# Half-row transposes with one copy per unit, GpSimd's weight split cut by stage, a reversed second branch, and one operation moved from VectorE to ScalarE, in a two-block transformer kernel

## The chip, the cores and the metric

The kernel is one program on one core of a Trainium2 chip. A core has TensorE (PE in the profile; PEld is its weight load), VectorE (DVE), ScalarE (ACT), GpSimd (POOL) and SyncE (SP), which runs the queue of the weight DMAs. The metric is the device time of one execution in microseconds (us). What a measurement of this kernel can tell from no change is about 0.2%, some 4 us.

## The reference

The input is one sequence of 512 tokens with 1024 channels, in float32. Two layers of a first block are followed by one layer of a second.

```python
for l in range(2):                                   # first block
    h = rmsnorm(x, attn_norm[l])
    q, kc, vc, ksl, vsl, kwn, vwn, gts, gq, gk, gv, ga, gr, uv = split(h @ w_in[l])
    o_nsa = gates-weighted sum of three attentions   # compressed, selected, window
    o_gla = gated linear attention(gq, gk, gv, ga, gr)
    o_sg = spatial gating(uv)
    x = x + concat([o_nsa, o_gla, o_sg]) @ w_out[l]
    h = rmsnorm(x, ffn_norm[l])
    x = x + (silu(h @ w_gate[l]) * (h @ w_up[l])) @ w_down[l]
x = rmsnorm(x, final_norm)
h = rms_norm(x, g_pre) * (1 + scl) + shift           # second block
xa, za, q, k, v, zb, ga, gb = split(h @ w_in_2)
y_a = (recurrence(xa) + reversed recurrence(xa)) * silu(za) @ w_pa
y_b = neighbourhood attention(q, k, v) * silu(zb) @ w_pb
x = x + gate * ((sigmoid(ga) * y_a + sigmoid(gb) * y_b) @ w_o)
return rms_norm(x, g_final)
```

With 8 selection blocks and a top-k of at least 8, the selected attention of the first block is a full causal attention, and so is the window attention (the window is 512). Each has 8 heads of 64 channels, and the softmax of each is multiplied by a gate for its row.

## The kernel before

**Weights.** All large products run over a stream of 278 slots of 128x1024 weights (`stream_plan`), in a ring of four (`RING`). SyncE loads a slot into `raw`, GpSimd splits it in two parts that TensorE can multiply in its fast float32 form: `w_hi` is the rounded weight (line 2079, a product with ones), and `w_lo` is what rounding lost (line 2083). The activations are split likewise (`a_hi` by ScalarE, `a_lo` by VectorE at line 1410). A product of a 128x128 weight tile is then three matmuls (lines 402, 405 and 406), and a slot of eight tiles is 24. The first matmul of a slot raises `slot_used`, which frees the slot before it, so GpSimd starts on slot n+4 when TensorE starts on slot n+1. `pieces_of` decides for each turn of the ring: where a slot stands beside much VectorE work, four pieces of 256 columns each for `w_hi` and then for `w_lo`, and else one piece of 1024 columns each. GpSimd's program is written with hardware loops over turns.

**The order of the work.** Nothing is scheduled by a tool. `ORDER`, `BEFORE` and `BESIDE` name, step by step, which projection runs beside which part of the linear attention and of the softmax attention, and each engine runs its program in that order. PSUM has eight banks. `claim` and `room` hand a bank out and make TensorE wait until its last reader has raised `free`. In the projections `aux_bank` takes the banks in turn, first of 4, from "Nh" on of 7 (`pool_of`). The first projection, `gate`, is always in bank 0, and every eviction waits for `rstd`, the factor of the norm, which is ready only when TensorE is through with the first projection and the sum of squares (line 427).

**The first block's attention** runs over 32 units u in each layer: head pair j = u // 8, row block i = u // 2 % 4, and branch u % 2 (selected or window). A unit has w = 128 * (i + 1) keys. For each unit and each of two heads TensorE makes scores (line 641), VectorE the maximum (1620), ScalarE the exponentials (1125), VectorE the scaling by 1/sum and the gate (1669), TensorE a transpose of each 128x128 block (653) in bank 4 (head 0) or 5 (head 1), ScalarE a copy to SBUF (1146), and TensorE the product with v (691), which adds into bank 6 over all eight units of a head pair. TensorE is two units ahead with the scores and one behind with the values. After the last unit of a pair, ScalarE copies bank 6 out (1177), and the next pair's first product (685) waits for that. ScalarE's further work in this loop, the exponentials of the compressed branch (1133) and the activations of other mixers (1170), stands between.

**The gates.** `gN` holds the gates with a row of tokens on each partition. ScalarE writes it (1005), and VectorE then multiplies eight columns by `rowok` (1472), since the first rows have no compressed key.

**The second block** makes its transposes of softmax rows (835) already on halves of 64 rows, the upper into bank 4 and the lower into bank 5.

## Time and profile before

| | |
|---|---|
| median of 3 runs | 2053.39 us (2050.51 to 2055.06) |
| the profiled execution | 2054.61 us, its span 2052.6 us |
| granted clock of TensorE, mean | 0.969 of full speed |
| busy: PE, POOL, DVE, ACT | 94%, 69%, 57%, 30% of the span |
| layer 1 of the first block, from the first evictions to the attention's end | about 729 to 1010 us |

Start and duration in the timeline are in us; "[5.06 <-DVE proj L1504]" says that the engine had stood idle for 5.06 us and what ended that. A row with x8 is eight instructions in one go, and its duration reaches from the first start to the modelled end of the last, so the pace of matmuls is read from one start to the next start. Line numbers are those of the kernel before.

### The profile page before, as it was taken

How to read it: one execution, taken by the hardware profiler on the slowest of the kernel's cores; microseconds unless marked ns; L12 is line 12 of the kernel's file. 1: busy time of each engine (PE TensorE's matmuls, PEld its weight loads, DVE VectorE, ACT ScalarE, POOL GpSimd, SP SyncE). 2: the span in 40 equal slices, each digit the busy share in tenths (PEclk: the TensorE clock that was granted, in tenths of full speed). 3: DMA queues.
4: the chain of work that ended last, by engine and by line, in shares of the span. 5: the costliest groups of instructions: out<-in, count | busy, mean ns of one | idle time of the engine just before them, and what ended most of it. 6: DMA issues, size and time to landing. Idle time of an engine off the chain costs nothing.

```text
span 2052.6 us, 28491 instructions
## 1 busy us (share of the span) xinstructions
PE 1924.2 (94%) x10022; PEld 1489.2 (73%) x10022; DVE 1160.2 (57%) x1670; ACT 615.6 (30%) x1116; POOL 1419.6 (69%) x1208
## 2 busy tenths in 40 slices
PE   7898889999999999988899999997999999989997
PEld 5676557888888877755588888885777777768775
DVE  5765774466257347478556704654937666650353
ACT  4124662210011131266531100113036566540111
POOL 8554117988789985511298978886897878757772
PEclk9999989999999999999999999998999999999998
DMA  5132002343334222300124433542132233222221
GB/s 204 53 96 80 22 11 83 122 143 108 97 121 136 92 72 81 116 21 22 32 93 123 133 100 96 148 124 67 51 108 84 79 94 87 76 72 93 84 91 41
DMA packets 68680, 182.44 MB, mean 89 GB/s; under 512 B 23888, under 2 KB 24144, under 8 KB 68432
## 3 DMA queue, kind: packets, MB, share of 16 engines
q1 hardware_dynamic: 60480, 154.48, 24.8%
q10 hardware_dynamic: 8080, 26.32, 4.1%
q8 instruction: 80, 1.31, 0.3%
q14 instruction: 40, 0.33, 0.1%
HBM read 178.67 MB, written 2.10 MB: 88 GB/s over the span
## 4 chain that ended last, share of the span: by engine, by line
PE 70%; DVE 13%; ACT 7%; issue 6%; POOL 2%; DMA 1%; ACTq 0%; DVEq 0%; POOLq 0%
PE PS L402 21%; PE PS L406 20%; PE PS L405 20%; POOL w_lo L2083 2%; PE PS L691 1%; PE PS L653 1%; PE PS L641 1%; PE PS L441 1%; ACT P L1251 1%; ACT rg L1322 1%; DVE gN L1472 1%; DVE P L1946 1%; PE PS L538 1%; POOL w_hi L2079 1%; DVE PS L1620 1%
## 5 line engine op out<-in xcount | busy, mean ns | idle before, releaser
L2079 POOL TENSOR_TENSOR w_hi<-raw,const 128x256 fp32r<-128x256 f32 (+1 forms) x602 | 641.9, 1088 | 586.1 <-PE PS L402 578.2
L2083 POOL TENSOR_TENSOR w_lo<-raw,w_hi 128x256 fp32r<-128x256 f32 (+1 forms) x602 | 783.9, 1324 | 13.4
L402 PE MATMUL PS<-a_hi,w_hi 128*128 128x512 f32 x1616 | 651.7, 403 | 42.3 <-POOL w_lo L2083 14.1
L405 PE MATMUL PS<-a_lo,w_hi 128*128 128x512 f32 x1616 | 635.8, 393 | 0.0
L406 PE MATMUL PS<-a_hi,w_lo 128*128 128x512 f32 x1616 | 635.3, 393 | 0.0
L402 PEld LDWEIGHTS PS<-a_hi,w_hi 128*128 128x128 f32 x1616 | 307.1, 190 | 128.6 <-issue 46.0
L406 PEld LDWEIGHTS PS<-a_hi,w_lo 128*128 128x128 f32 x1616 | 307.2, 190 | 65.9
L405 PEld LDWEIGHTS PS<-a_lo,w_hi 128*128 128x128 f32 x1616 | 307.6, 190 | 64.8 <-issue 3.4
L1793 DVE TENSOR_TENSOR work<-PS,rstd 128x512 f32<-128x512 f32 x88 | 60.8, 691 | 147.6 <-PE PS L406 140.9
L402 PE MATMUL PS<-f_hi,w_hi 128*128 128x512 f32 x352 | 138.7, 394 | 0.0
L406 PE MATMUL PS<-f_hi,w_lo 128*128 128x512 f32 x352 | 138.0, 392 | 0.0
L405 PE MATMUL PS<-f_lo,w_hi 128*128 128x512 f32 x352 | 136.6, 388 | 0.0
L1216 ACT ACTIVATE work<-work 128x512 f32<-128x512 f32 x44 | 27.8, 633 | 314.4 <-DVE small L1797 314.3
L1849 DVE TENSOR_TENSOR x<-PS,x 128x512 f32<-128x512 f32 x32 | 22.1, 691 | 158.4 <-PE PS L406 158.3
L1804 DVE TENSOR_TENSOR f_lo<-work,f_hi 128x512 fp32r<-128x512 f32 x44 | 85.5, 1944 | 36.9 <-ACT f_hi L1219 36.9
L1219 ACT ACTIVATE f_hi<-work 128x512 fp32r<-128x512 f32 x44 | 27.9, 634 | 205.1 <-DVE work L1800 205.1
L1800 DVE TENSOR_TENSOR work<-work 128x512 f32<-128x512 f32 x44 | 83.5, 1898 | 2.8 <-ACT work L1216 1.4
L653 PEld LDWEIGHTS PS<-const,work 128*128 128x128 f32 x320 | 37.7, 152 | 63.7 <-DVE work L1669 43.3
L653 PE MATMUL PS<-const,work 128*128 128x128 f32 x320 | 58.2, 310 | 24.8 <-DVE work L1669 21.7
L406 PEld LDWEIGHTS PS<-f_hi,w_lo 128*128 128x128 f32 x352 | 66.1, 188 | 15.5
L405 PEld LDWEIGHTS PS<-f_lo,w_hi 128*128 128x128 f32 x352 | 66.1, 188 | 14.8
L1620 DVE CUSTOM_DVE_ANT_0 PS<-PS,before_diag 128x128 f32<-128x128 f32 (+3 forms) x128 | 63.9, 499 | 21.3 <-PE PS L641 17.4
(290 smaller groups left out, 2494.1 us busy)
## 6 DMA issues: line engine op xcount, KB each, us to landing
raw<-weights SPq DMA_DIRECT2D x278, 512.0 KB, 3.5
work<-mod_w ACTq DMA_DIRECT2D x24, 512.0 KB, 3.6
work<-cmp_w ACTq DMA_DIRECT2D x8, 1024.0 KB, 5.6
bias<-rpb SPq DMA_DIRECT2D x256, 12.0 KB
rgw<-rgw ACTq DMA_DIRECT2D x8, 256.0 KB, 2.6
out<-xc SPq DMA_DIRECT2D x8, 256.0 KB, 2.0
const<-const SPq DMA_DIRECT2D x1, 1436.5 KB, 15.3
x<-x_t SPq DMA_DIRECT2D x4, 256.0 KB, 6.8
```

Source lines behind the costliest of these rows:

```text
L402: ins = nc.tensor.matmul(out, wh, hi, start=start, stop=False)
L405: nc.tensor.matmul(out, wh, lo, start=False, stop=False)
L406: return nc.tensor.matmul(out, wl, hi, start=False, stop=stop)
L653: ins = nc.tensor.transpose(PS[:, 4 + hh, n * P:(n + 1) * P], work[:, 2 * br + hh, n * P:(n + 1) * P], ident)
L1216: A(work[:, f % 2, :], work[:, f % 2, :], ACT.Silu).then_inc(to_dve.sem, 1)
L1219: A(f_hi[:, f, :], work[:, 4 + f % 2, :], ACT.Copy).then_inc(h_hi.sem, 1)
L1620: V.tensor_tensor_reduce(s2[:, hh, 0:w], s2[:, hh, 0:w], mask, -1.0, -2 * NEG_MASK, ALU.add, ALU.min, nmax[:, br, hh:hh + 1]).then_inc(max ...
L1793: TT(work[:, w0 + f % 2, :], PS[:, b0 + f % 2, :], rstd[:, :], ALU.mult)\
L1800: TT(work[:, 4 + f % 2, :], work[:, f % 2, :], work[:, 2 + f % 2, :], ALU.mult)\
L1804: TT(f_lo[:, f, :], work[:, 4 + f % 2, :], f_hi[:, f, :].bitcast(F32), ALU.subtract)\
L2079: G.tensor_tensor(w_hi[:, r, k, :], raw[:, r, k, :], ones[:, k, :], ALU.mult).then_inc(pool_chain, 1)
L2083: ins = G.tensor_tensor(w_lo[:, r, k, :], raw[:, r, k, :], w_hi[:, r, k, :].bitcast(F32), ALU.subtract)
```

## The change

- `row_block`: in the window branch (odd u) the row blocks come in reverse. The widths of the units were 1, 1, 2, 2, 3, 3, 4, 4 times 128 and are 1, 4, 2, 3, 3, 2, 4, 1.
- `turn`: each 128x128 transpose is two of 64 rows, the upper into bank 4 and the lower into bank 5. Both heads lie in both banks, one semaphore counts them, and ScalarE copies both banks with one instruction.
- `pool_of["next"] = 0` at the start of each layer.
- The copy of bank 6 stands ahead of the compressed exponentials and the activations in ScalarE's loop.
- The multiplication of `gN` by `rowok` is ScalarE's (a copy with a scale for each partition).
- GpSimd has no loops. `parts_of` gives each slot its pieces, and every piece waits until the one before it is complete: (2, 4), two of `w_hi` with a tensor_scalar and four of `w_lo`; (2, 2), two of each in turn; (1, 1), as before. By the plan 85 slots are (2, 4), 49 are (2, 2) and 144 are (1, 1), where before 108 had four and four and 170 one and one.

```diff
+def row_block(u):
+    i = u // 2 % NT
+    return i if u % 2 == 0 else NT - 1 - i
...
-                pool_of["banks"] = 4
+                pool_of["banks"], pool_of["next"] = 4, 0
...
                     j, i, br = unit(u)
+                    key = (l, "PT", u)
+                    if claim(key, 4):
+                        pe.wait_ge(*room(key))
+                    if u == 0:
+                        pe.wait_ge(free[5], fills[5])
                     for hh in range(2):
                         pe.wait_ge(scaled.sem, scaled.seen_by("pe"))
-                        key = (l, "PT", hh, u)
-                        if claim(key, 4 + hh):
-                            pe.wait_ge(*room(key))
                         for n in range(i + 1):
-                            ins = nc.tensor.transpose(PS[:, 4 + hh, n * P:(n + 1) * P],
-                                                      work[:, 2 * br + hh, n * P:(n + 1) * P], ident)
-                        ins.then_inc(filling(key)[0], 1)
+                            for r in range(2):
+                                q = slice(HD * r, HD * r + HD)
+                                ins = nc.tensor.transpose(PS[:, 4 + r, (2 * n + hh) * HD:(2 * n + hh + 1) * HD],
+                                                          work[q, 2 * br + hh, n * P:(n + 1) * P], ident[q, q])
+                    ins.then_inc(filling(key)[0], 1)
...
-                                                   work[:, 4 + 2 * br + hh, n * P:(n + 1) * P],
+                                                   turned[:, :, (2 * n + hh) * HD:(2 * n + hh + 1) * HD],
...
                         A(gN[:, :, :], PS[:, uses[(l, name, "T")][0], 0:NT * 24].rearrange("p (n c) -> p n c", c=24), ACT.Sigmoid)\
+                            .then_inc(act_chain.sem, 1)
+                        act.wait_ge(act_chain.sem, act_chain.raised())
+                        if l == 0:
+                            act.wait_ge(const_in, 16)
+                        A(gN[:, 0, 2:24:3], gN[:, 0, 2:24:3], ACT.Copy, scale=c_("rowok"))\
                             .then_inc(emptied((l, name, "T")), 1)
...
-                        g = gN[:, 0, 2:24:3]
-                        TS(g, g, c_("rowok"), None, ALU.mult).then_inc(dve_chain.sem, 1)
-                        dve.wait_ge(dve_chain.sem, dve_chain.raised())
...
-                    for hh in range(2):
-                        act.wait_ge(*filling((l, "PT", hh, u)))
-                        A(work[:, 4 + 2 * par + hh, 0:w], PS[:, 4 + hh, 0:w], ACT.Copy)\
-                            .then_inc(emptied((l, "PT", hh, u)), 1)
-                        act.wait_ge(*emptying((l, "PT", hh, u)))
+                    act.wait_ge(*filling((l, "PT", u)))
+                    A(work[:, 4 + 2 * par:6 + 2 * par, 0:w], PS[:, 4:6, 0:w], ACT.Copy)\
+                        .then_inc(emptied((l, "PT", u)), 1)
+                    act.wait_ge(*emptying((l, "PT", u)))
...
+            def split(n, hi_parts, lo_parts):
+                r = n % RING
+                pool.wait_ge(raw_in[r], 16 * (n // RING + 1))
+                if n >= RING:
+                    pool.wait_ge(slot_used, n - RING + 1)
+                each, per = 8 // hi_parts, lo_parts // hi_parts
+                for h in range(hi_parts):
+                    k = slice(h * each, (h + 1) * each)
+                    if hi_parts == lo_parts:
+                        G.tensor_tensor(w_hi[:, r, k, :], raw[:, r, k, :], ones[:, k, :], ALU.mult).then_inc(pool_chain, 1)
+                    else:
+                        G.tensor_scalar(w_hi[:, r, k, :], raw[:, r, k, :], 1.0, None, ALU.mult).then_inc(pool_chain, 1)
+                    pool.wait_ge(pool_chain, counted())
+                    for q in range(h * per, (h + 1) * per):
+                        k = slice(q * 8 // lo_parts, (q + 1) * 8 // lo_parts)
+                        ins = G.tensor_tensor(w_lo[:, r, k, :], raw[:, r, k, :], w_hi[:, r, k, :].bitcast(F32), ALU.subtract)
+                        if q < lo_parts - 1:
+                            ins.then_inc(pool_chain, 1)
+                            pool.wait_ge(pool_chain, counted())
                 ins.then_inc(split_done, 1)
...
+            def parts_of(n):
+                kind, m = PLAN[n][0], PLAN[n][-1]
+                if n == 0 or kind in ("pa", "pb", "wo") or kind == "in2" and not KT <= m < 6 * KT:
+                    return 2, 2
+                if kind in ("in", "in2") or kind == "out" and m < 2:
+                    return 2, 4
+                return 1, 1
```

In the rows of the programs below, a name ahead of the arrow is what is written, and the shape is that of the output. First ScalarE in layer 0, from the copy of unit 16's transposes to that of unit 17's (line 1177, after it 1159, is the copy of bank 6; 1170 and 1180 are the activations). Before:

```order
L1146 ACTIVATE work<-PS 128x128 x2
L1125 ACTIVATE work,sums<-PS,nmax 128x256 x2
L1133 ACTIVATE Pc<-Pc 128x8x31
L1170 ACT_TABLE_LOAD
L1170 ACTIVATE proj<-proj 128x512 x2
L1177 ACTIVATE proj<-PS 128x512
L1146 ACTIVATE work<-PS 128x128 x2
```

After:

```order
L1150 ACTIVATE work<-PS 128x2x128
L1130 ACTIVATE work,sums<-PS,nmax 128x256 x2
L1159 ACTIVATE proj<-PS 128x512
L1138 ACTIVATE Pc<-Pc 128x8x31
L1180 ACT_TABLE_LOAD
L1180 ACTIVATE proj<-proj 128x512 x2
L1150 ACTIVATE work<-PS 128x1024
```

The copy of bank 6 moved ahead of three other operations, two copies became one, and unit 17 is four blocks wide where it was one.

Then TensorE in layer 0, from unit 14's transposes to unit 16's (653 transposes, 691 values, 641 and then 637 scores). Before:

```order
L653 MATMUL PS<-const,work 128x128 x8
L691 MATMUL PS<-work,proj 64x128 x6
L641 MATMUL PS<-keys,proj 128x128 x2
L653 MATMUL PS<-const,work 128x128 x8
L691 MATMUL PS<-work,proj 64x128 x8
L641 MATMUL PS<-keys,proj 128x256 x2
L653 MATMUL PS<-const,work 128x128 x2
```

After:

```order
L653 MATMUL PS<-const,work 128x64 x16
L691 MATMUL PS<-work,proj 64x128 x4
L637 MATMUL PS<-keys,proj 128x512 x2
L653 MATMUL PS<-const,work 128x64 x4
L691 MATMUL PS<-work,proj 64x128 x8
L637 MATMUL PS<-keys,proj 128x256 x2
L653 MATMUL PS<-const,work 128x64 x4
```

Each transpose became two with half the output columns, and the width changes from unit to unit in place of every second one.

Last GpSimd at layer 0's output projection, the slots "out" 6, "out" 7 and the first of the feed-forward part. Before:

```order
L2079 TENSOR_TENSOR w_hi<-raw,const 128x1024 [waits slot_used,raw_in3]
L2083 TENSOR_TENSOR w_lo<-raw,w_hi 128x1024 [waits pool_chain]
L2079 TENSOR_TENSOR w_hi<-raw,const 128x256 [waits slot_used,raw_in0]
L2079 TENSOR_TENSOR w_hi<-raw,const 128x256 x3
L2083 TENSOR_TENSOR w_lo<-raw,w_hi 128x256 [waits pool_chain] x4
L2079 TENSOR_TENSOR w_hi<-raw,const 128x256 [waits slot_used,raw_in1]
```

After:

```order
L2086 TENSOR_TENSOR w_hi<-raw,const 128x1024 [waits slot_used,raw_in3]
L2092 TENSOR_TENSOR w_lo<-raw,w_hi 128x1024 [waits pool_chain]
L2086 TENSOR_TENSOR w_hi<-raw,const 128x1024 [waits slot_used,raw_in0]
L2092 TENSOR_TENSOR w_lo<-raw,w_hi 128x1024 [waits pool_chain]
L2086 TENSOR_TENSOR w_hi<-raw,const 128x1024 [waits slot_used,raw_in1]
```

Four slots of eight pieces each (two are shown in part) are slots of two pieces after the change. The same holds in layer 1.

## Rows read from the trace of the kernel before

**Rows 1.** The page, section 1: busy us, share of the span, instructions.

```profile
PE 1924.2 (94%) x10022; PEld 1489.2 (73%) x10022; DVE 1160.2 (57%) x1670; ACT 615.6 (30%) x1116; POOL 1419.6 (69%) x1208
```

**Rows 2.** Windows: stretch, length, busy of each engine, PEclk, DMA, GB/s.

```profile
26.20:85.26 59.06, 50.27 (x289) 39.06 (x288) 37.46 (x32) 17.90 (x25) 43.63 (x67) 0.89 0.24 72
730.30:778.31 48.01, 47.97 (x287) 37.79 (x288) 24.62 (x31) 13.60 (x19) 39.62 (x56) 0.94 0.23 68
195.00:305.00 110.00, 92.20 (x632) 59.09 (x630) 81.65 (x231) 76.46 (x186) 15.78 (x24) 0.91 0.05 15
1500.00:1835.00 335.00, 323.15 (x1869) 243.90 (x1868) 212.45 (x320) 195.80 (x327) 262.26 (x323) 0.99 0.30 85
```

**Rows 3.** Timeline at layer 1's start, VectorE and TensorE: start, duration, instruction.

```profile
729.39 0.69 DVE L1504 TENSOR_TENSOR proj<-PS,rstd 128x512 f32<-128x512 f32 x1 [5.38 <-ACT rstd L987]
...
730.34 0.76 PE L402 MATMUL PS<-a_hi,w_hi 128*128 128x512 f32 x1 [5.06 <-DVE proj L1504]
...
735.60 0.43 PE L402 MATMUL PS<-a_hi,w_hi 128*128 128x512 f32 x1
...
737.02 0.40 PE L402 MATMUL PS<-a_hi,w_hi 128*128 128x512 f32 x1
```

**Rows 4.** Timeline, the `rowok` operation and what follows, layers 0 and 1.

```profile
41.95 16.55 DVE L1472 TENSOR_SCALAR gN<-gN,const 128x8 f32<-128x8 f32 x1 [0.93 <-ACT gN L1005]
...
55.65 2.82 POOL L2083 TENSOR_TENSOR w_lo<-raw,w_hi 128x256 fp32r<-128x256 f32 x4
...
67.47 1.99 PE L538 MATMUL PS<-work 32*128 32x64 f32 x32 [7.54 <-DVE work L1524]
...
746.86 0.48 DVE L1472 TENSOR_SCALAR gN<-gN,const 128x8 f32<-128x8 f32 x1 [0.95 <-ACT gN L1005]
```

**Rows 5.** Timeline of TensorE: transposes of the first and second block.

```profile
212.74 1.09 PE L653 MATMUL PS<-const,work 128*128 128x128 f32 x8
213.76 1.09 PE L691 MATMUL PS<-work,proj 128*64 128x128 f32 x16
...
1618.50 0.71 PE L835 MATMUL PS<-const,P 64*128 64x64 f32 x16
1619.14 0.50 PE L402 MATMUL PS<-a_hi,w_hi 128*128 128x512 f32 x1
```

**Rows 6.** Waits of TensorE over the span: us in total, times, longest.

```profile
PE PS L685 <- ACT proj L1177: 11.8, 4, 4.3
...
PE PS L402 <- DVE y_lo L2038: 2.9, 2, 1.8
```

**Rows 7.** Timeline of layer 0's unit 16, ScalarE and TensorE.

```profile
254.36 0.60 ACT L1177 ACTIVATE proj<-PS 128x512 f32<-128x512 f32 x1
...
255.01 2.07 PE L685 MATMUL PS<-PTc,vblk 64*128 64x512 f32 x2 [4.29 <-ACT proj L1177]
```

**Rows 8.** GpSimd's groups by shape: busy us, mean ns, idle before.

```profile
L2083 POOL TENSOR_TENSOR w_lo<-raw,w_hi 128x1024 fp32r<-128x1024 f32 x170 | 428.8, 2522 | 13.4
L2083 POOL TENSOR_TENSOR w_lo<-raw,w_hi 128x256 fp32r<-128x256 f32 x432 | 355.1, 853 | 0.0
L2079 POOL TENSOR_TENSOR w_hi<-raw,const 128x1024 fp32r<-128x1024 f32 x170 | 347.4, 2044 | 320.5 <-PE PS L402 318.4
L2079 POOL TENSOR_TENSOR w_hi<-raw,const 128x256 fp32r<-128x256 f32 x432 | 294.4, 712 | 265.6 <-PE PS L402 259.8 <-DMA const<-const 5.8
```

**Rows 9.** Timeline, a VectorE operation beside a piece of 1024 columns.

```profile
1379.18 2.74 POOL L2083 TENSOR_TENSOR w_lo<-raw,w_hi 128x1024 fp32r<-128x1024 f32 x1
...
1379.69 2.79 DVE L1397 TENSOR_TENSOR work<-work 128x512 f32<-128x512 f32 x1
```

**Rows 10.** Timeline at the feed-forward part's start in layer 0.

```profile
357.76 0.69 DVE L1778 TENSOR_TENSOR x<-PS,x 128x512 f32<-128x512 f32 x1 [2.53 <-PE PS L406]
...
361.71 1.11 DVE L1383 TENSOR_TENSOR tmp<-tmp,sq 128x512 f32<-128x512 f32 x1
...
362.97 1.10 PE L427 MATMUL PS<-tmp,const 128*128 128x512 f32 x2
```

More of the change, by code:

```diff
@@ L102 @@
              + [(m, k) for m in range(OUT_EARLY, KT) for k in range(KT)])
-PIECES = 4
-def beside_vector(item):
-    if item[0] == "in2":
-        return item[1] < 6 * KT
-    return item[0] == "in" or item[0] == "gate" and item[2] < 2
+def row_block(u):
+    i = u // 2 % NT
+    return i if u % 2 == 0 else NT - 1 - i
 def stream_plan():
@@ L1172, in _ @@
                             act.wait_ge(to_dve.sem, to_dve.raised())
-                    if u % 8 == 0 and u:
-                        t = u // 8 - 1
-                        act.wait_ge(*filling((l, "O", t)))
-                        A(proj[:, t, :], PS[:, 6, :], ACT.Copy).then_inc(emptied((l, "O", t)), 1)
-                        act.wait_ge(*emptying((l, "O", t)))
                     if CONVERT_FROM <= u < U - 1:
@@ L2067, in _ @@
             G = nc.gpsimd
+            spent = [0]
             ones = c_("ones")[:, 0:1].unsqueeze(2).to_broadcast([P, 8, P])
-            def split(r, arrival, used, chain, pieces):
-                pool.wait_ge(raw_in[r], arrival)
-                if used is not None:
-                    pool.wait_ge(slot_used, used)
-                each = 8 // pieces
-                for n in range(pieces):
-                    k = slice(n * each, (n + 1) * each)
-                    G.tensor_tensor(w_hi[:, r, k, :], raw[:, r, k, :], ones[:, k, :], ALU.mult).then_inc(pool_chain, 1)
-                for n in range(pieces):
-                    k = slice(n * each, (n + 1) * each)
-                    pool.wait_ge(pool_chain, chain + n + 1)
-                    ins = G.tensor_tensor(w_lo[:, r, k, :], raw[:, r, k, :], w_hi[:, r, k, :].bitcast(F32), ALU.subtract)
-                ins.then_inc(split_done, 1)
@@ L2086, in pieces_of, with counted @@
[L2086 to L2109 removed]
+            def counted():
+                spent[0] += 1
+                return spent[0]
@@ L2112, in _ @@
+            def parts_of(n):
[5 more added lines that the diff above has]
+                return 1, 1
+            pool.wait_ge(head_in, 16)
+            for n in range(SLOTS):
+                split(n, *parts_of(n))
         @block.sync
```

46 lines of the change are left out of this document (14 added, 32 removed).

## The prediction

> **What bounds the kernel now.** I read the page first. TensorE is busy for 94% of the span [rows 1], so the time is TensorE's work, its gaps, and the slower pace behind gaps. Then I read windows by stage. The feed-forward parts are full of TensorE's work, and nothing shorter on another engine helps there. In the second block's main stage TensorE is busy for 323 of 335 us, and GpSimd for 262. In the first block's attention TensorE has 92 of 110 us, VectorE 82 and ScalarE 76 [rows 2]: three engines that hand each unit on to one another, none of them full. Last I followed each gap of TensorE over 2 us to what ended it. Two lie at the starts of the layers and one at each fourth or so of the attention; the rest belongs to serial norms that the change doesn't touch.
>
> A gap costs twice. At layer 1's start TensorE stood for 5.06 us, and the 12 matmuls behind the gap took from 730.34 to 735.60 us, 0.44 us each (the level of 1.2 GHz), while the next six took 1.42 us, 0.24 each (2.4 GHz) [rows 3]. So the gap cost another 12 x 0.20 = 2.4 us.
>
> **Step A, banks reset at layer 1.** The 42 bank picks of a layer leave `next` at 3, so layer 1's second projection gets bank 0, in which the first one still waits for `rstd`. The row shows it: TensorE started right after the eviction of 729.39 [rows 3]. With `next` at 0 it gets bank 1 and needn't wait, as in layer 0. Gain 5.1 + 2.4 = 7.5 us. What is late next is the norm factor itself, which is there 5 us before TensorE is through with the second projection.
>
> **Step B, `rowok` on ScalarE.** In layer 0 this operation on eight columns took 16.55 us, from 41.95 until 58.50, and GpSimd's row of pieces without a gap ended at 58.47; in layer 1 the same operation took 0.48 us [rows 4]. While it stood, evictions and the linear attention's first level stood behind it, and TensorE waited 7.54 us for the latter, at a low clock behind that [rows 4]. To price it I compare the same stretch of both layers, from the second projection's first matmul to the doubling of the keys: 59.06 us and 48.01 us [rows 2]. The difference, 11.0 us, holds everything, the clock included. The operation on ScalarE costs a few tenths ahead of an exponential chain that VectorE meets just in time. The small tensor_scalar operations that follow on VectorE could stall likewise; they took under 0.6 us in layer 1, beside busy GpSimd pieces, and now the pieces have pauses. Against that, a `w_hi` piece of 512 columns holds VectorE's two-input operations longer than one of 256, a dozen of them at some 0.1 us. I take 10 us (bounds 0, if another operation stalls in its place, and 11).
>
> **Step C, the attention.** Halves: eight whole transposes took from 212.74 to 213.76, 0.128 us each; 16 half ones in the second block took from 1618.50 to 1619.14, 0.040 each [rows 5]. A block of 128x128 now costs 0.080 in place of 0.128, and there are 160 in a layer: 7.7 us less work of TensorE a layer. It is worth all of that only where TensorE is what the others wait for. VectorE and ScalarE are as loaded as it, so I take a quarter, 2 us a layer. Copy of bank 6: TensorE waited for it 11.8 us in four places, two in each layer [rows 6]. At a pair's first unit the copy now stands ahead of everything that delayed it. At unit 16 the wait was 4.29 us, and the copy at 254.36 stood behind table loads and activations [rows 7]. These still stand ahead of the next unit's exponentials, so TensorE does some 2.3 us of products inside the old gap and then waits for those. The gap halves, and the slow stretch behind it goes: the product there took 2.07 us. I take 4 us a layer. Merged copies: at 0.2 us of fixed cost each, ScalarE is relieved by 6 us a layer, but a copy now starts after both heads and not after the first. Reversed branch: all engines' work for two units in a row is constant, where before two wide ones followed each other; waits between the three get shorter in one place and longer in another. I take nothing for either, with -3 to +4 us a layer as bounds. Sum 6 us a layer, 12 in all (bounds -4 and 31: nothing but the merged copies' loss, or all of the transposes' 15.4, the 11.8 and a gain from the balance).
>
> **Step D, finer pieces at the end.** The slots of `pa`, `pb`, `wo` and the last of `in2` go from pieces of 1024 to 512 columns, in the stretch where VectorE makes `y_lo` and TensorE waited 2.9 us for it [rows 6]. I take 2 us (0 to 5).
>
> **Step E, coarser pieces at the feed-forward part's start.** This is the part that costs. The four slots that GpSimd splits while the output projection ends had eight pieces each and now have two. A VectorE operation with two SBUF inputs gets in only between pieces: started at 1379.69 beside a piece that ran until 1381.92, it ended at 1382.48, 0.56 later [rows 9]. The Trainium skill says the same on its page "SBUF — State Buffer", section "Who interferes with whom": the pair of ports is locked for a whole instruction, so the second to come blocks fully; the trace agrees, by that row. In this stretch VectorE has for each of eight tiles one free addition (0.7) and two such operations. Before, the last was done at 362.8, and TensorE's sum of squares followed at 362.97 with no gap [rows 10]. Now two get in per slot of 5.5 us, one behind `w_hi` (2.0) and one behind `w_lo` (2.5) [rows 8]. Walking tile by tile from 336: tile 1 is done at 341.3, 2 at 346.8, 3 at 352.1, 4 at 357.6, 5 at 363.1, and 6 and 7, with GpSimd idle by then, at 365.3 and 366.8. The first feed-forward product, started at 357.7, needs `a_lo` of tile 6 at 361.8 and gets it at 364.5, and ends at 366.8 in place of 362.9. Loss 3.9 us and with even chance a slow stretch of 2.4 as in [rows 3]: 5 us a layer, 10 in all (bounds 0, if the operations slip in more often, and 14).
>
> **Step F, GpSimd's speed.** A slot of eight pieces took 5.15 us undisturbed, of which the start of a piece is about 0.1 us, and with VectorE beside it 4 x (0.71 + 0.85) = 6.2 on the mean [rows 8]. TensorE takes 5.5 us for a slot at least. A (2, 4) slot has two pieces fewer and five pauses (0.08 us each, 13.4 us for 170 slots [rows 8]). `w_hi` by tensor_scalar isn't in the trace. The nearest row is the tensor_tensor for `w_hi`, 2.0 us a slot; as bounds I take half of that and twice that, 1.0 and 4.0. I take the row itself, so a slot costs 0.2 us more, hidden at seven or more us per slot in both projection stages. At layer 0's start GpSimd is at most one slot behind its old times while TensorE has 9 us of slack by its fifth slot.
>
> **Sum.** 7.5 + 10 + 12 + 2 - 10 = 21.5 us less than the profiled execution's 2054.6 us, 2033 us. That execution lay 1.2 us above the median of the runs, so I predict 2032 us for the median.
>
> **The rivals.**
> 1. *The gains of the layer starts hold and the attention pays in full.* The attention pays 20 us in place of 12, since most of the halves' 15.4 becomes time, and step E costs 5 in place of 10: 21.5 + 8 + 5 = 34.5 us less, 2019 us. For it: the attention has 18 us of gaps in 110 [rows 2], and slow stretches behind several of them. Against it: VectorE has 82 us of work there and would be the next bound. Chance 0.22.
> 2. *The attention pays nothing.* TensorE's shorter work turns into longer waits for VectorE, at a low clock, and step E costs its 14: 17.5 + 2 - 14 + 0 = 5.5 us less, 2048 us. For it: nearly all of TensorE's gaps there are ended by another engine. Chance 0.20.
> 3. *GpSimd becomes the bound*, the one that ends slower. The place is the second block's main stage, 335 us for some 43 slots, 7.7 us each, in which GpSimd is busy for 262 us [rows 2], 6.0 a slot. From 1.7 us more per slot on, TensorE waits for it. Pauses take 0.2, so the point is a tensor_scalar of 3.5 us for 1024 columns in place of 2.0. At 4.0 each of 43 slots would be 0.5 late, 22 us, and the layers' starts lose as much as they gain from step B: 2032 + 22 + 10 = 2064 us. The page "GPSIMD Engine Reference" of the Trainium skill, section "Elementwise — side-by-side cycle accounting", puts the cost of two inputs down to one read port shared by them, and by it one input is faster than two; no run here shows it. By that rule this rival falls away. Chance 0.08.
> 4. *The stall of step B only moves* to another small VectorE operation, and step E costs 14: 21.5 - 10 - 4 = 7.5 us less, 2046 us. Chance 0.07.
>
> My forecast has the remaining 0.43, with its own range of 2025 to 2041. The range for all reaches from 2014 to 2050. A measurement of this kernel tells 0.2%, 4 us, from no change. Faster by more than that is all but rival 3 and an edge of rivals 2 and 4: 0.86. Within it: 0.05. Slower: 0.09.
>
> **What would show it.** In the profile after: no gap at layer 1's second projection (A); the stretch from the second projection to the keys' doubling at 48 us or less in both layers (B); no wait of TensorE for the copy of bank 6 above 2.5 us, and the attention's window shorter by some 6 us (C); VectorE's operations at 2.3 to 2.8 us each between the output projection and the feed-forward part, and TensorE waiting 3 to 4 us there (E); the tensor_scalar of 512 columns near 1.0 us (F). I am wrong if it is above 1.7 us, if TensorE's first feed-forward product has no gap, or if the attention got shorter by more than 12 us a layer.

## The result, and the profile after

The changed kernel takes 2030.8 us (median of 4 runs, 2029.0 to 2032.2); the kernel before, measured beside it, 2053.9 us (4 runs). The ratio is 0.989 with a 95% interval of 0.987 to 0.991: faster by 23 us. The forecast was 2032 us. So the sum came out right. Its terms did not all: the attention's was twice too large, the last stage's a third of what was measured, and the largest gain is due to another part of the change than the prediction named. That the sum is so near is in part luck.

The profiled execution took 2030.9 us, its span 2028.8. Section 1 of the page of the profile, against [rows 1]:

```profile
PE 1905.6 (94%) x10342; PEld 1484.7 (73%) x10342; DVE 1149.1 (57%) x1668; ACT 605.5 (30%) x1054; POOL 1446.2 (71%) x998
```

GpSimd's groups by shape, against [rows 8] (busy us, mean ns, idle before):

```profile
L2092 POOL TENSOR_TENSOR w_lo<-raw,w_hi 128x1024 fp32r<-128x1024 f32 x144 | 364.5, 2531 | 11.3
...
L2092 POOL TENSOR_TENSOR w_lo<-raw,w_hi 128x256 fp32r<-128x256 f32 x340 | 269.7, 793 | 27.5
L2088 POOL TENSOR_SCALAR w_hi<-raw 128x512 fp32r<-128x512 f32 x170 | 268.0, 1577 | 162.5 <-PE PS L398 155.1
...
L2086 POOL TENSOR_TENSOR w_hi<-raw,const 128x512 fp32r<-128x512 f32 x98 | 110.2, 1124 | 73.8 <-PE PS L398 64.4 <-DMA const<-const 5.6
```

TensorE has 320 instructions more (the halves) and is busy 19 us less; its share of the span is the same. The 512-column tensor_scalar took 1.58 us, not the assumed 1.0.

**Where the time came from.** Both programs run the same projections, so the same matmul can be looked up in the two TensorE timelines, and the difference of its starts says what was gained up to there (from here on, such a difference is called a mark, and its size is in us):

| the same matmul, place | before | after | gained |
|---|---|---|---|
| layer 0, second projection | 33.51 | 31.79 | 1.7 |
| layer 0, keys' doubling | 85.53 | 71.96 | 13.6 |
| layer 0, ahead of the attention | 166.59 | 152.90 | 13.7 |
| layer 0, output projection | 334.60 | 319.25 | 15.4 |
| layer 0, feed-forward part | 691.53 | 681.82 | 9.7 |
| layer 1, third projection | 739.53 | 722.03 | 17.5 |
| layer 1, ahead of the attention | 820.17 | 802.51 | 17.7 |
| layer 1, output projection | 1031.36 | 1009.97 | 21.4 |
| layer 1, feed-forward part | 1388.87 | 1372.60 | 16.3 |
| second block, last stage's start | 1837.32 | 1819.73 | 17.6 |
| end | 2024.81 | 2001.07 | 23.7 |

So the layers' starts gave 13.6 and 7.8 us, the attention 1.7 and 3.7, the last stage 6.1; the feed-forward parts' starts took 5.7 and 5.1 back. The first 1.7 us are no gain of the new pieces: experiments 1 and 2, which keep the old ones, show 1.3 and 1.2 at the same matmul. The windows that answer to [rows 2] (stretch, length, busy of each engine, granted clock, DMA share, GB/s) are below; that from 195 us lies some 14 us later in the attention's course than the one before, since all comes earlier:

```profile
25.45:71.70 46.25, 46.25 (x289) 36.27 (x288) 22.44 (x31) 18.94 (x26) 43.29 (x44) 0.99 0.26 81
195.00:305.00 110.00, 91.86 (x781) 62.84 (x778) 82.21 (x226) 67.29 (x151) 16.00 (x11) 0.84 0.07 20
715.00:760.80 45.80, 45.80 (x289) 36.05 (x288) 23.79 (x31) 17.94 (x24) 42.92 (x43) 1.00 0.25 81
```

The stretch from the second projection to the keys' doubling is TensorE's own work, with no gap, in both layers: 46.25 and 45.80 us, where it had been 59.06 and 48.01. Layer 1's start against [rows 3], TensorE's timeline:

```profile
714.55 1.02 PE L423 MATMUL PS<-tmp,const 128*128 128x512 f32 x2
715.00 0.80 PE L398 MATMUL PS<-a_hi,w_hi 128*128 128x512 f32 x1
715.64 0.40 PE L401 MATMUL PS<-a_lo,w_hi 128*128 128x512 f32 x1
...
718.17 0.39 PE L398 MATMUL PS<-a_hi,w_hi 128*128 128x512 f32 x1
```

The second projection follows the statistics at once, at 0.23 us a matmul. Step E's place in layer 0, against [rows 10] (GpSimd, VectorE, TensorE):

```profile
342.69 1.90 POOL L2086 TENSOR_TENSOR w_hi<-raw,const 128x1024 fp32r<-128x1024 f32 x1 [0.79 <-PE PS L398]
344.66 2.70 POOL L2092 TENSOR_TENSOR w_lo<-raw,w_hi 128x1024 fp32r<-128x1024 f32 x1
...
343.21 1.92 DVE L1414 SCALAR_TENSOR_TENSOR a_lo<-x,misc,a_hi 128x512 fp32r<-128x512 f32 x1
345.17 2.74 DVE L1387 TENSOR_TENSOR tmp<-tmp,sq 128x512 f32<-128x512 f32 x1
...
349.48 0.50 PE L398 MATMUL PS<-a_hi,w_hi 128*128 128x512 f32 x1 [3.04 <-DVE a_lo L1414]
350.99 0.79 PE L398 MATMUL PS<-a_hi,w_hi 128*128 128x512 f32 x1 [0.55 <-DVE a_lo L1414]
352.43 1.87 PE L423 MATMUL PS<-tmp,const 128*128 128x512 f32 x2
```

VectorE gets in once behind each piece: 1.92 us behind `w_hi`, 2.74 behind `w_lo`. TensorE stands 3.6 us, and the sum of squares lasts 1.87 in place of 1.10. TensorE's waits over the span, against [rows 6] (us, times, longest):

```profile
PE PS L653 <- DVE work L1669: 26.8, 24, 3.9
...
PE PS L398 <- DVE a_lo L1414: 10.3, 8, 3.1
...
PE PS L653 <- ACT work L1150: 6.1, 3, 3.0
...
PE PS L673 <- ACT proj L1167: 4.0, 2, 2.0
```

The 11.8 us for the copy of bank 6 are gone. Other waits grew instead: that for the scaling was 21.7 us (17 times, longest 3.4), and that for ScalarE's copy of the transposes (line 1150) was 1.5. Most of the latter lies at unit 16, where this copy now stands behind the table load and the activations:

```profile
239.79 1.29 ACT L1180 ACTIVATE proj<-proj 128x512 f32<-128x512 f32 x2
241.11 1.02 ACT L1150 ACTIVATE work<-PS 128x1024 f32<-128x1024 f32 x1
242.19 0.69 PE L653 MATMUL PS<-const,work 64*128 64x64 f32 x8 [2.98 <-ACT work L1150]
```

### The profile page after: what moved, and what is told of

Same layout as the page of the kernel before. It is cut to its first block, busy times and chain, and to the rows that moved or that the text cites. A ratio compares the mean times of both kernels' runs of the same rounds, so it can differ in the third digit from the quotient of the medians.

```text
span 2028.8 us, 27919 instructions
## 1 busy us (share of the span) xinstructions
PE 1905.6 (94%) x10342; PEld 1484.7 (73%) x10342; DVE 1149.1 (57%) x1668; ACT 605.5 (30%) x1054; POOL 1446.2 (71%) x998
## 4 chain that ended last, share of the span: by engine, by line
PE 68%; DVE 19%; ACT 8%; issue 4%; DMA 1%; ACTq 0%; DVEq 0%
PE PS L398 21%; PE PS L402 20%; PE PS L401 20%; DVE tmp L1387 2%; DVE a_lo L1414 2%; DVE xc L1907 1%; PE PS L437 1%; ACT P L1255 1%; DVE work L1669 1%; DVE PS L1620 1%; ACT rg L1326 1%; DVE rg L1964 1%; PE PS L534 1%; DVE rg L1967 1%; PE PS L691 1%
## 5 line engine op out<-in xcount | busy, mean ns | idle before, releaser
L2092 POOL TENSOR_TENSOR w_lo<-raw,w_hi 128x256 fp32r<-128x256 f32 (+2 forms) x582 | 773.8, 1329 | 46.5
L2086 POOL TENSOR_TENSOR w_hi<-raw,const 128x1024 fp32r<-128x1024 f32 (+1 forms) x242 | 406.1, 1678 | 340.8 <-PE PS L398 328.9
L2088 POOL TENSOR_SCALAR w_hi<-raw 128x512 fp32r<-128x512 f32 x170 | 268.0, 1577 | 162.5 <-PE PS L398 155.1
L653 PEld LDWEIGHTS PS<-const,work 64*128 64x128 f32 x640 | 34.2, 157 | 64.9 <-issue 43.5
L398 PEld LDWEIGHTS PS<-f_hi,w_hi 128*128 128x128 f32 x352 | 66.2, 188 | 13.2
```

Source lines behind the costliest of these rows:

```text
L398: ins = nc.tensor.matmul(out, wh, hi, start=start, stop=False)
L653: ins = nc.tensor.transpose(PS[:, 4 + r, (2 * n + hh) * HD:(2 * n + hh + 1) * HD], work[q, 2 * br + hh, n * P:(n + 1) * P], ident[q, q])
L2086: G.tensor_tensor(w_hi[:, r, k, :], raw[:, r, k, :], ones[:, k, :], ALU.mult).then_inc(pool_chain, 1)
L2088: G.tensor_scalar(w_hi[:, r, k, :], raw[:, r, k, :], 1.0, None, ALU.mult).then_inc(pool_chain, 1)
L2092: ins = G.tensor_tensor(w_lo[:, r, k, :], raw[:, r, k, :], w_hi[:, r, k, :].bitcast(F32), ALU.subtract)
```

## The experiments

The kernel before had medians of 2054.4 us beside experiments 1 to 4, 2054.1 beside 5 to 8 and 2054.5 beside 9 to 12; the last four ran on another chip. Each ratio is to the kernel before, with its 95% interval. Where two changed kernels are compared with each other, both intervals count (each some 0.17% to either side, so 4 to 5 us together, an estimate from them): differences below that rest on the marks alone, and marks come from one execution each.

**1. A and B alone, on the kernel before.**

```diff
-                pool_of["banks"] = 4
+                pool_of["banks"], pool_of["next"] = 4, 0
...
-                        TS(g, g, c_("rowok"), None, ALU.mult).then_inc(dve_chain.sem, 1)
...
+                        A(gN[:, 0, 2:24:3], gN[:, 0, 2:24:3], ACT.Copy, scale=c_("rowok"))\
```

> The kernel before, with two parts of the change alone: banks reset at layer 1 (A) and rowok on ScalarE (B). Theory, from the two traces' marks: TensorE's place after the key doubling of layer 0 is 11.9 us earlier by B and after layer 1's second projection another 7.8 us by A, and nothing gives it back: 2053.9 - 19.7 = 2034 us. Rival: part of B's gain came from the pauses that GpSimd's pieces now have, so that with the old pieces another small VectorE operation stalls in rowok's place; then only A's 7.8 stays, 2046 us, and an operation of layer 0 at 40 to 60 us shows 10 us or more.

Measured: 2046.4 us, ratio 0.9966 (0.9954 to 0.9977). The rival. VectorE in layer 0:

```profile
44.69 0.69 DVE L1506 TENSOR_TENSOR proj<-PS,rstd 128x512 f32<-128x512 f32 x1 [4.94 <-PE PS L406]
45.57 13.55 DVE L1561 SCALAR_TENSOR_TENSOR work<-decay,work 128x512 f32<-128x512 f32 x1 [0.19 <-ACT work L1018]
59.16 1.23 DVE L1563 TENSOR_TENSOR_SCAN decay<-const,work 128x512 f32<-128x512 f32 x1
```

With `rowok` gone from VectorE, the next operation with its inputs in SBUF is shut out for 13.55 us, until the same point. The evictions from PSUM at 37.95 and 44.69 passed beside the same row of pieces in 0.69 us. A's part stands: TensorE's marks gain 7.3 us over the start of layer 1, and nothing in layer 0.

**2. GpSimd's part as before, in the changed kernel** (D, E and F undone, and with them the pauses; the hardware loops are back).

```diff
-            for n in range(SLOTS):
-                split(n, *parts_of(n))
...
+                    with pool.Fori(first, last) as i:
+                        for r in range(RING):
+                            split(r, i * 16 + 16, i * RING + (r - RING + 1),
+                                  i * (RING * n) + (chain + (r - RING * first) * n), n)
```

> The changed kernel with GpSimd's part as before (eight pieces or two, no pauses, no tensor_scalar): D, E and F undone. Theory: VectorE's operations at the feed-forward part's start go back to 1.1 us and the gaps of 3.6 us go (10.7 us for both layers), the finer pieces' 6.1 us at the end are lost: 2030.8 - 10.7 + 6.1 = 2026 us. Rival: the pauses carry part of step B, and a stall of some 10 us comes back in layer 0: 2036 us.

Measured: 2041.8 us, 0.9944 (0.9926 to 0.9962). The rival again: the same operation takes 13.19 us from 45.68. By the marks nothing is lost at the feed-forward parts' starts (E undone), and the last stage gains 1.6 us in place of 6.1 (D undone).

**3. The attention as before, in the changed kernel** (C undone: `row_block`, `turn`, `values` and ScalarE's loop as in the minus lines of the diff above).

> The changed kernel with the first block's attention as before (whole transposes, two copies a unit, bank 6's copy behind the other work, the second branch not reversed): C undone in full. Theory, from the marks: the attention gave 1.7 us in layer 0 and 3.9 in layer 1, so 2030.8 + 5.6 = 2036 us. Rival: the marks mix C with the new pieces beside it, and C is worth its forecast of 12: 2043 us.

Measured: 2036.4 us, 0.9922 (0.9904 to 0.9940). C is worth 5.6 us in all, not 12; the marks of the two attentions say 6.1.

**4. E alone undone.**

```diff
+                if kind == "out" and m == KT - 1 or kind == "gate" and m < 2 or kind == "up" and m == 0:
+                    return 4, 4
                 return 1, 1
```

> The changed kernel with four slots of each layer (the last of out, the first two of gate, the first of up) in eight pieces of 256 columns instead of two of 1024, which undoes E alone. Theory: VectorE's operations there last 1.1 us in place of 1.9 and 2.8, the gap of TensorE ahead of the first feed-forward product goes in both layers: 2030.8 - 10.7 = 2020 us. Rival: eight pieces with pauses cost GpSimd about 1 us a slot more than the slot's 5.5 us of TensorE, so that TensorE waits for GpSimd instead and half is kept: 2025 us.

Measured: 2016.5 us (2015.9 to 2018.2), 0.9821 (0.9803 to 0.9838): the fastest of all. VectorE and TensorE there:

```profile
342.95 0.75 DVE L1414 SCALAR_TENSOR_TENSOR a_lo<-x,misc,a_hi 128x512 fp32r<-128x512 f32 x1
343.74 0.98 DVE L1387 TENSOR_TENSOR tmp<-tmp,sq 128x512 f32<-128x512 f32 x1
...
346.04 0.39 PE L398 MATMUL PS<-a_hi,w_hi 128*128 128x512 f32 x1
346.27 0.39 PE L401 MATMUL PS<-a_lo,w_hi 128*128 128x512 f32 x1
```

No gap is left, and by the marks 5.6 us come in layer 0 and 5.3 in layer 1. A further 3 us come in the second block, where this kernel has no edit. Nearly all of them (2.7) lie around one wait of TensorE for VectorE's `qkv`: it is 1.2 us shorter here, and the matmuls behind it run at 2.4 GHz, where in the changed kernel the first eight ran at 1.2 GHz (0.43 us each in place of 0.23). First the changed kernel, then this one; the last two rows are the windows over the wait and the matmuls behind it:

```profile
1483.72 0.62 PE L398 MATMUL PS<-a_hi,w_hi 128*128 128x512 f32 x1 [2.96 <-DVE qkv L1981]
1470.63 0.50 PE L398 MATMUL PS<-a_hi,w_hi 128*128 128x512 f32 x1 [1.81 <-DVE qkv L1981]
...
1480.50:1491.30 10.80, 7.84 (x28) 6.12 (x27) 3.09 (x3) 1.26 (x2) 10.06 (x11) 0.84 0.24 84
1468.50:1476.70 8.20, 6.39 (x28) 4.99 (x27) 2.01 (x3) 1.29 (x2) 7.63 (x9) 1.00 0.29 101
```

Why VectorE is ready earlier there isn't known.

**5. The copy of bank 6 late again**: its six lines back behind `if u in BESIDE` and the activations of `if u in (16, 25)`.

> The changed kernel with ScalarE's copy of bank 6 again behind the other work of its unit; halves, merged copies and the reversed branch stay. Theory: the copy's place is what C is worth; TensorE waits 4 us for it at unit 16 of each layer again, with a slow product behind: 2030.8 + 5 = 2036 us. Rival: the wait only goes over to the next unit's exponentials and weights, since the activations between are the same either way: 2031 to 2032 us.

Measured: 2038.3 us, 0.9924 (0.9909 to 0.9939), 7.5 us slower than the changed kernel. TensorE waits 4.9 and 5.0 us for the copy in the two layers, and the attentions lose 5.0 and 1.7 us by the marks.

**6. Whole transposes.**

```diff
-                                ins = nc.tensor.transpose(PS[:, 4 + r, (2 * n + hh) * HD:(2 * n + hh + 1) * HD],
-                                                          work[q, 2 * br + hh, n * P:(n + 1) * P], ident[q, q])
+                            ins = nc.tensor.transpose(PS[:, 4 + hh, n * P:(n + 1) * P],
+                                                      work[:, 2 * br + hh, n * P:(n + 1) * P], ident)
...
-                                                   turned[:, :, (2 * n + hh) * HD:(2 * n + hh + 1) * HD],
+                                                   turned[:, hh, n * P:(n + 1) * P],
```

> The changed kernel with whole 128x128 transposes in place of the halves; copy of both banks in one, early copy and reversal stay. Each block costs TensorE 0.128 us again in place of 0.080, 15.4 us in 320 blocks. Theory: most of it was spent waiting for VectorE's scaling, a third or so is time: 2030.8 + 4 = 2035 us. Rival 1 of the prediction (the attention pays in full): 2046 us. Rival 2 (it pays nothing): 2031 us.

Measured: 2030.5 us, 0.9887 (0.9867 to 0.9907): the halves give nothing that can be told from zero, and the marks of the two attentions differ by 0.5 us one way and 0.4 the other. The windows of the two attentions, first of the changed kernel, then of this one:

```profile
162.00:300.00 138.00, 114.04 (x967) 78.63 (x967) 105.16 (x292) 88.87 (x195) 27.13 (x23) 0.88 0.07 20
848.00:990.00 142.00, 116.86 (x982) 81.67 (x981) 106.29 (x293) 89.31 (x197) 29.75 (x26) 0.88 0.07 20
```

```profile
162.00:300.00 138.00, 118.05 (x807) 78.14 (x807) 105.95 (x293) 88.92 (x196) 27.08 (x23) 0.91 0.07 20
848.00:990.00 142.00, 121.85 (x825) 81.00 (x824) 106.45 (x293) 89.22 (x197) 30.27 (x26) 0.92 0.06 20
```

With halves TensorE is busy 4 and 5 us less in the same time, and the granted clock is 0.88 in place of 0.91 and 0.92. VectorE has the same 105 to 106 us. The saved work became waiting (in these windows TensorE stands 9.0 us longer with halves, 4.6 of them in waits for the scaling), and the granted clock is lower. Over the whole span TensorE is busy 8.8 us less with halves (1905.6 and 1914.4), not the 15.4 that the prediction counted.

**7. Two copies a unit.**

```diff
-                    A(work[:, 4 + 2 * par:6 + 2 * par, 0:w], PS[:, 4:6, 0:w], ACT.Copy)\
+                    A(work[:, 4 + 2 * par, 0:w], PS[:, 4, 0:w], ACT.Copy).then_inc(act_chain.sem, 1)
+                    act.wait_ge(act_chain.sem, act_chain.raised())
+                    A(work[:, 5 + 2 * par, 0:w], PS[:, 5, 0:w], ACT.Copy)\
```

> The changed kernel with one copy of ScalarE for each of the two banks, as before, on the halved transposes; the second copy can't start earlier than with one, since each bank gets its last half at the end. So only the cost of a second instruction on ScalarE, 0.2 us for each of 64 units, is added: 2031 us if ScalarE isn't what the attention waits for, 2030.8 + 64 x 0.2 = 2044 us if it is.

Measured: 2032.8 us, 0.9903 (0.9884 to 0.9922), 2 us slower and inside the uncertainty. The 13 us that ScalarE's extra instructions would cost if the attention waited for it are excluded.

**8. No reversal.**

```diff
-    i = u // 2 % NT
-    return i if u % 2 == 0 else NT - 1 - i
+    return u // 2 % NT
```

> The changed kernel with the second branch's row blocks in the order 0 to 3 again, so that two wide units follow each other. Theory, the forecast's: it moves waits from one unit to another and is worth nothing, 2031 us. Rival a: the balance is what keeps TensorE fed, and without it VectorE's scaling is late in each wide pair, some 4 us a layer: 2039 us. Rival b: the reversal costs, because the new waits for the exponentials (3.0 us, twice) and the longer ones for the scaling (26.8 us in place of 21.7) come with it: 2026 us.

Measured: 2035.4 us, 0.9910 (0.9894 to 0.9926), 4.6 us slower, which is at the edge of what these runs can tell. The marks of the two attentions lose 3.9 and 4.3 us, but the profiled execution took 2039.9 us, 4.5 more than the median, so they overstate it. The reversal is worth something, between the forecast's nothing and rival a, and how much is open.

**9. Pauses, on the kernel before.** GpSimd waits for each piece; their size, number and order stay, `rowok` stays on VectorE. One thing more goes with it: the hardware loops of GpSimd's program are written out, as in the changed kernel.

```diff
                     G.tensor_tensor(w_hi[:, r, k, :], raw[:, r, k, :], ones[:, k, :], ALU.mult).then_inc(pool_chain, 1)
+                    pool.wait_ge(pool_chain, counted())
...
+                    if q < pieces - 1:
+                        ins.then_inc(pool_chain, 1)
+                        pool.wait_ge(pool_chain, counted())
...
-                    with pool.Fori(first, last) as i:
...
+            for n in range(SLOTS):
+                split(n, pieces_of(n // RING))
```

> The kernel before with one edit: GpSimd waits after each of its pieces until it is done, and their number, size and order stay; rowok stays on VectorE. Theory formed after the first four runs: VectorE's operation with SBUF operands alone is shut out by a row of pieces issued without a pause, whichever operation it is, and the pauses end that: no operation of VectorE above 2 us at 40 to 60 us, and 2053.9 - 11 = 2043 us (the 24 or so pauses of 0.1 us before the fifth slot may cost 1 of 12). Rival: it was the larger or fewer pieces (512 columns, tensor_scalar) that broke the row; then 13 to 17 us of stall are still there and the time is 2054 us.

Measured: 2041.2 us, 0.9941 (0.9925 to 0.9958), 13.3 us faster. The time is the theory's, and by the marks 11.9 us come between layer 0's second projection and the keys' doubling. VectorE's timeline:

```profile
39.64 0.54 DVE L1472 TENSOR_SCALAR gN<-gN,const 128x8 f32<-128x8 f32 x1 [0.93 <-ACT gN L1005]
43.62 0.69 DVE L1504 TENSOR_TENSOR proj<-PS,rstd 128x512 f32<-128x512 f32 x1 [3.44 <-PE PS L406]
44.34 0.69 DVE L1559 SCALAR_TENSOR_TENSOR work<-decay,work 128x512 f32<-128x512 f32 x1
```

`rowok` takes 0.54 us where it took 16.55 [rows 4].

The traces hold more shut-outs than that of layer 0. In the second block's main stage of the kernel before, two operations of VectorE take 5.23 and 5.25 us where their shortest take 1.22 and 0.89, and the second ends at 1545.95, 0.55 us behind the end of GpSimd's row (VectorE, GpSimd):

```profile
1540.70 5.25 DVE L1961 SCALAR_TENSOR_TENSOR rg<-asq,rg 128x512 f32<-128x512 f32 x1
...
1542.59 2.81 POOL L2083 TENSOR_TENSOR w_lo<-raw,w_hi 128x256 fp32r<-128x256 f32 x4
```

Experiments 1 and 2 have such operations there too (up to 4.1 and 8.5 us). In no traced kernel with pauses does any operation of VectorE take more than 2.5 us above its shortest.

What this leaves open is the loops. All these shut-outs lie beside GpSimd code in a hardware loop, and each kernel with pauses also has the loops written out, so no run tells the two apart. The loop by itself doesn't shut VectorE out: beside looped rows without a pause it got in as well (VectorE, GpSimd):

```profile
1401.95 0.99 DVE L1397 TENSOR_TENSOR work<-work 128x512 f32<-128x512 f32 x1
...
1402.35 3.27 POOL L2083 TENSOR_TENSOR w_lo<-raw,w_hi 128x256 fp32r<-128x256 f32 x4
```

**10. Experiment 4, and finer pieces in the second block's first projection.**

```diff
+                if kind == "in2" and m < KT:
+                    return 4, 4
```

> The changed kernel with eight pieces in the four slots of each layer as in the run that undid E alone (2016.5 us), and in the eight slots of the second block's first projection too, which had four pieces of 512. VectorE's operations there took 1.42 and 1.65 us beside the pieces of 512 and 1.0 to 1.1 beside those of 256. Theory: TensorE's waits for a_lo (3.1 us) and the slow products between go down by some 2 us, and the 3.0 us for qkv at 1483 don't change: 2014 to 2015 us. Rival: the stage is bounded by VectorE's chain before it and nothing comes: 2016.5 us.

Measured: 2023.0 us, 0.9847 (0.9830 to 0.9864), 6.5 us slower than experiment 4. Both the theory and the rival fell. VectorE's operations did go to 0.98 and 1.10 us, but now GpSimd is late in this stage. TensorE's waits from 1390 to 1500 us:

```profile
PE PS L398 <- POOL w_lo L2092: 3.6, 5, 1.4
PE PS L398 <- DVE a_lo L1886: 2.1, 4, 0.5
```

In experiment 4 it didn't wait for GpSimd there. The marks show some 5 us lost in this stage; another 2 to 3 come behind it, most of them between 1781 and 1809 us, with no edit there, and stay unexplained.

**11. tensor_tensor for the 512-column `w_hi`, and coarse pieces at the end.**

```diff
-                        G.tensor_scalar(w_hi[:, r, k, :], raw[:, r, k, :], 1.0, None, ALU.mult).then_inc(pool_chain, 1)
+                        G.tensor_tensor(w_hi[:, r, k, :], raw[:, r, k, :], ones[:, k, :], ALU.mult).then_inc(pool_chain, 1)
...
-                if n == 0 or kind in ("pa", "pb", "wo") or kind == "in2" and not KT <= m < 6 * KT:
+                if n == 0 or kind == "in2" and m < KT:
                     return 2, 2
+                if kind in ("pa", "pb", "wo") or kind == "in2" and m >= 6 * KT:
+                    return 1, 1
```

> The changed kernel with two edits in different stages, told apart by TensorE's marks. (i) w_hi of the (2, 4) slots by tensor_tensor with ones in place of tensor_scalar (F): 1.12 in place of 1.58 us for 512 columns, 0.9 us a slot less of GpSimd's time; theory: hidden but for layer 0's first slots, 0 to 1 us by the end of layer 1; rival: tensor_scalar's longer pieces held VectorE, 3 us. (ii) The last stage's slots in pieces of 1024 again (D undone): theory from the marks 6 us lost between 1810 us and the end; rival: D is worth its forecast of 2. Sum by the theories 2030.8 - 0.5 + 6 = 2036 us; by the forecast for D 2032 us.

Measured: 2050.8 us, 0.9985 (0.9976 to 0.9994): 20 us slower than the changed kernel. The marks put 4.7 us into the last stage (D), and 14.2 ahead of it: 7.3 until layer 1's attention (3.8 of them before layer 0's second projection) and 5.3 in the second block's main stage. GpSimd's operation is shorter by itself:

```profile
L2088 POOL TENSOR_TENSOR w_hi<-raw,const 128x512 fp32r<-128x512 f32 x170 | 189.3, 1113 | 233.7 <-PE PS L398 226.9
```

but VectorE takes longer for the same work: in the main stage, taken from the same matmul to the same matmul, it is busy 183.2 us (1552.2 to 1823.4) where it was 171.8 (1543.3 to 1809.7), and TensorE waits 10.7 us there for ScalarE's `P` in place of 5.7. The difference is seen best at layer 0's start. First the changed kernel, then this one:

```profile
19.57 1.93 POOL L2088 TENSOR_SCALAR w_hi<-raw 128x512 fp32r<-128x512 f32 x1
20.19 0.98 DVE L1414 SCALAR_TENSOR_TENSOR a_lo<-x,vec,a_hi 128x512 fp32r<-128x512 f32 x1
21.20 0.69 DVE L1387 TENSOR_TENSOR tmp<-tmp,sq 128x512 f32<-128x512 f32 x1
```

```profile
16.18 1.37 POOL L2088 TENSOR_TENSOR w_hi<-raw,const 128x512 fp32r<-128x512 f32 x1
16.69 1.41 DVE L1414 SCALAR_TENSOR_TENSOR a_lo<-x,vec,a_hi 128x512 fp32r<-128x512 f32 x1
```

The operation of 20.19 ends at 21.17, inside the piece that lasts until 21.50. Of six such operations started beside a tensor_scalar in the first 30 us, three ended inside it and the other three took 0.69 us; of 9 beside a tensor_tensor there, and of 14 in this kernel, none ended inside. The whole traces say the same of VectorE's two-input operations on 512 columns in SBUF: in the changed kernel 26 of 42 that started inside a tensor_scalar ended inside it, and none of 222 inside a tensor_tensor; in this kernel none of 243.

**12. The late copy and no reversal together.**

> The changed kernel with both the late copy of bank 6 and the second branch not reversed. Alone they cost 7.5 and 4.6 us, and all of C undone cost 5.6. Theory: the parts stand in for each other, since without the reversal the unit behind a pair's first is narrow and a late copy holds up less: 2030.8 + 5.6 = 2036 us or a little more. Rival: they add up, 2043 us, and it is the whole transposes or the two copies that make up for it in the old form.

Measured: 2039.4 us, 0.9927 (0.9911 to 0.9945), 8.6 us slower than the changed kernel. That is midway between the theory (5.6) and the sum (12.1), and with the uncertainty of a comparison it decides for neither. The marks of the two attentions lose 6.7 us by the late copy, 8.2 without the reversal, 10.7 with both, and 6.1 with all of C undone. By them both are true: the parts stand in for each other, and whole transposes and two copies regain 4 to 5 us in the old form. There the copy of the first head can run while the second is transposed; that this is the reason wasn't tried by itself.

## Why the prediction was right in its sum, and where its steps failed

- **A** (7.5 us): right. The marks show 7.8, and experiment 1 gave 8.0 as a whole, with nothing from B.
- **B** (10 us): the size was right (11.9 by the marks), the step failed: "The small tensor_scalar operations that follow on VectorE could stall likewise; they took under 0.6 us in layer 1, beside busy GpSimd pieces, and now the pieces have pauses." The move gives nothing; the next operation of VectorE stalls in its place (13.55 us, experiment 1), as rival 4 had it. GpSimd's new form gives it, with `rowok` where it was (experiment 9): pieces with a pause between, in a program without hardware loops. The end of the stall with the row speaks for the pauses; the loops weren't tried apart. The prediction had the clue in its hands: it noted that the stall ended at 58.50 with GpSimd's row at 58.47. It took the operation for the cause, and the pauses for a side remark. Rival 4 didn't come about only because the same change held the cure, which is luck: the sign given for B, the stretch at 48 us or less, came true for another reason than the one stated.
- **C** (12 us): mis-sized, 5.6 measured. The early copy was forecast at 8 for both layers and is worth 7.5 by itself; the halves were forecast at 4 and are worth nothing that can be told from zero, since TensorE's waits there grew by what its work shrank; the reversal was put at nothing and is worth 4.6, at the edge of the uncertainty, the merged copies 2, inside it. They don't add up: together they bring 5.6. At unit 16 the step foresaw a wait for the exponentials; what TensorE waits for there, 2.98 us, is the copy of the transposes, which stands ahead of them and behind the same activations.
- **D** (2 us): too small. The marks give 6.1 for the last stage, and taking D back costs 4.7 of them (experiment 11) and 4.5 (experiment 2). The rest isn't D's: experiment 9 gains 1.4 there with the old pieces. The step priced one wait of [rows 6], and neither the slow matmuls behind it nor the other operations of VectorE in that stage; which of them made D larger wasn't tried apart.
- **E** (-10 us): right in place, mechanism and size: operations of 1.9 and 2.8 us, a gap of 3.6 us, 5.7 and 5.1 us lost by the marks. Undoing it gave 14.4, of which 11 lie there and 3 around the wait for `qkv`, which no term had. The Trainium skill's page "SBUF — State Buffer", section "Who interferes with whom", calls the shared pair of ports an exclusive lock; its words that the lock holds for a whole instruction stand beside VectorE's two-port modes. Beside tensor_tensor pieces these rows bear the rule out for two inputs: VectorE's 1.92 and 2.74 us end 0.5 to 0.6 us behind the pieces' ends.
- **F** (0): the duration was wrong, 1.58 us in place of 1.0, so a slot's `w_hi` costs 3.15 us; that stayed under the 3.5 us from which GpSimd would have become the bound (rival 3). The term came out at about nothing (13.6 to 13.7 us through layer 0's linear attention, 17.5 to 17.7 in layer 1), for a reason that the prediction lacked: a longer piece that doesn't shut VectorE out. The same sizes by tensor_tensor cost some 14 us (experiment 11). In the second block 3.0 us go behind the wait for `qkv` (the marks fall from 17.0 to 14.0 by 1497 us, in experiment 9 by as much), and 3.6 come back by 1543 us, where the kernel before has the two shut-outs of 5.2 us. The prediction held rival 3 for void by a rule that one input is faster than two; here one input took 1.58 us and two took 1.11 (experiment 11), so it was the size of the slack that kept rival 3 away. Its means per slot are 7.8 and 6.1 us and not 7.7 and 6.0; the slack of 1.7 stands. The Trainium skill's page "SBUF — State Buffer", section "Who interferes with whom", says that a VectorE instruction with two SBUF inputs contends with a GpSimd instruction that reads SBUF. Beside a tensor_scalar, which reads SBUF, 26 of 42 ended before it did; there the measurement decides.

The measured terms: 1.7 + 11.9 + 7.8 + 5.4 + 6.1 - 10.8, and about 1.6 spread over the rest, make the 23.7 us of the marks, against a forecast of 21.5. D's and B's terms came out 6 us larger and C's 6.6 smaller, which nearly cancel, and 3.3 us (at the very start and spread) were in no term. The sum is right to 1.6 us by that luck.

## What to carry to other kernels

Where a small operation of one engine stalls, look at what the other engine was doing at the moment the stall ended, and treat that; here moving the operation only handed the stall to the next one. Cutting work on an engine that waits for others can be worth nothing: here 8.8 us less of TensorE's work gave no time that could be told from zero. Piece sizes are a trade with two sides in each stage: fine ones where VectorE feeds TensorE and GpSimd has time, coarser ones where GpSimd itself is late. With E undone, the change gives 37 us in place of 23.

## What was not expected of the hardware

- A VectorE operation with its inputs in SBUF can be shut out through a whole row of GpSimd's instructions issued without a pause (13.2 to 16.6 us in layer 0, up to 8.5 us in the second block), while operations that read PSUM pass in 0.69 us. With a wait between the pieces, about 0.08 us each, and the hardware loops written out, it doesn't occur. It isn't so in each row without pauses: at layer 0's very start, and beside the row of [rows 10], VectorE got in between such pieces (1.0 to 1.1 us an operation). These two rows are straight code, and all shut-outs lie beside looped code, but VectorE got in beside looped rows too (0.99 us at 1401.95). What decides was not found.
- GpSimd's tensor_scalar on 512 columns took 1.49 us undisturbed and 1.58 on the mean, its tensor_tensor with ones 1.11 on the mean (experiment 11); yet the slower one lets VectorE's two-input operations run beside it (26 of 42 ended inside a piece, against 0 of 222).
- Transposes in halves lowered TensorE's busy time by 4 to 5 us an attention, and the granted clock there was 0.88 in place of 0.91 and 0.92.
